# Attention of the 96-row heads: three key tiles to a turn in place of two

## The chip, the cores and the metric

The kernel runs on one core of a Trainium2 chip. The metric is the device time of one execution in microseconds (us), and of several executions the median. TensorE multiplies matrices, VectorE and ScalarE work elementwise and reduce, GpSimd (POOL) and SyncE (SP) here mostly issue transfers. TensorE's clock has two levels, 1.2 and 2.4 GHz; the profile gives the granted share of the higher one.

## The reference

A trunk of two layers works on 2048 latent tokens and 128 context tokens. In each layer one input projection feeds four groups of heads (latent attention, a state-space scan, a convolution module, grouped-query attention), whose outputs are gated and projected back. The change concerns the attention of the latent tokens to 128 context keys and 2048 latent keys, for four heads with 96 rows of query and key (64 plus 32 rotary) and four with 64:

```python
def one_block(qblk):
    s = jnp.einsum('bqgrd,bkgd->bgrqk', qblk, k).astype(jnp.float32) * scale
    p = jax.nn.softmax(s, axis=-1).astype(v.dtype)
    return jnp.einsum('bgrqk,bkgd->bqgrd', p, v)
```

## The kernel before

The function attention_phase runs once in each layer. Its unit is a block B: 1024 queries of one head, so two blocks for each of eight heads, 16 in a layer; blocks 0 to 7 are those of the 96-row heads (is_mla). A block walks over NKT = 17 tiles of 128 keys.

Each engine has its own program, written out in order, and they meet in semaphores. For a tile v of block B:

- scores(B, v) on TensorE: for a 96-row head six matmuls with 512 columns (two halves of the queries, three products each) into ST[unit % 2], two buffers of 1024 columns. It waits until the exponential of tile v - 2 has emptied its buffer.
- ScalarE takes the exponential of ST into Pb, five buffers. It waits until the value set and the sum of five tiles ago have used theirs.
- pv(B, v), the value set, on TensorE: the two query halves go side by side through two 64-column halves of the array into OT, in full float32. It waits for the exponential of its tile.
- add on VectorE sums the probabilities over the tiles into acc.

The exponential needs each query's maximum over all keys beforehand. So while block B is worked on, TensorE also computes raw scores of block B + 1 with queries on the partitions: fill(B + 1, r), r from 0 to 16, two matmuls with 512 columns (for r = 0, eight with 128) into the single buffer p1. VectorE reduces p1 to maxima. The next fill waits for it:

```python
out = p1
pe.wait_ge(q["red_done"], B * NKT + r + START)
```

VectorE's program takes, for each u from 0 to 16, reduce(B + 1, u) and then add(B, u - 1); behind u = 3 and 5 it sums the turned sums of block B - 1 (sum_keys), and in some blocks it splits a piece of the output weights behind u = 6 and 9.

TensorE's order in a block is the loop that the change touches: for u = 0, 2, 4, ... 16 a fill, the scores of tiles u and u + 1, some extra work, a second fill, and the value sets of tiles u - 2 and u - 1. At u = 0 the value set is that of tile 16 of the block before. Tile 16 has no second fill and no value sets; behind the loop come the value set of tile 14, max_row(B + 1) (eight transposes that make a row of the maxima) and the value set of tile 15. The extra work: turn_sums and turn transpose the sums and outputs of block B - 1 in turns u = 2, 4 and 6, and in blocks 0 and 1 of the first layer product does modulation rows for the next layer.

In block 0 no value set is carried over, so there the second fill of u = 0 and the first fill of u = 2 stand next to each other.

Of the kernel before, what the change touches and what calls it, by code (L numbers as in the profile page):

```python
# [29 lines left out]
DC = D // P  # L30
# [45 lines left out]
START = 1  # L76
# [1757 lines left out]
def attention_phase(nc, A, K, S, l, F, O, spare, M):  # L1834
# [7 lines left out]
    NKT = NLAT + 1  # L1842
# [10 lines left out]
    def is_mla(h):  # L1853
        return h < NMLA

    with ExitStack() as x:
# [27 lines left out]
        modulate = l == 0  # L1884
        if modulate:
            names += "bias_loaded m_used grown_ready m_row_ready g_stored m_stored m_loaded".split()
        q = {n: s.sem(n) for n in names}
# [3 lines left out]
        def loads(h, part):  # L1891
            return head_loads(l, h, part)
# [147 lines left out]
        def _(pe):  # L2040
            def fill(B, r):


                h, b = divmod(B, PER)
                par = h % 2
                if B == 0:
                    out = (p1, ST[1])[r % 2]
                    if r >= 2:
                        pe.wait_ge(q["red_done"], r - 1 + START)
                else:  # L2050
                    out = p1
                    pe.wait_ge(q["red_done"], B * NKT + r + START)
                if r == 0:
                    for i in range(NT_Q):
                        t = i // 2 + i % 2 * (NT_Q // 2)
                        q0 = b * QB + t * P
                        if is_mla(h):
                            qt, kt = Q1[par][0:QK, q0:q0 + P], K1[par][0:QK, LAT:KEYS]
                        elif t < NT_Q // 2:
                            qt, kt = Q1[par][0:HD, q0:q0 + P], K1[par][0:HD, LAT:KEYS]  # L2060
                        else:
                            qt, kt = Q2[par][HD:P, q0:q0 + P], K1[par][HD:P, LAT:KEYS]
                        mm = pe.matmul(out[:, t * P:(t + 1) * P], qt, kt, start=True, stop=True)
                else:
                    t, w = divmod(r - 1, WIDE)
                    q0 = b * QB + t * P
                    for c in range(2):
                        k0 = w * 1024 + c * 512
                        if is_mla(h):
                            qt, kt = Q1[par][0:QK, q0:q0 + P], K1[par][0:QK, k0:k0 + 512]  # L2070
                        elif c == 0:
                            qt, kt = Q1[par][0:HD, q0:q0 + P], K1[par][0:HD, k0:k0 + 512]
                        else:
                            qt, kt = Q2[par][HD:P, q0:q0 + P], K1[par][HD:P, k0:k0 + 512]
                        mm = pe.matmul(out[:, c * 512:(c + 1) * 512], qt, kt, start=True, stop=True)  # L2075
                mm.then_inc(q["p1_done"], 1)

            def context_scores():

                pe.wait_ge(q["c_summed"], 4 + START)  # L2080
                for h in range(NH):
                    rows = slice(0, QK if is_mla(h) else HD)
                    mm = pe.matmul(p1[:, h * P:(h + 1) * P], cQ[0][rows, h, :], cK[0][rows, h, :], start=True, stop=True)
                mm.then_inc(q["c_s_done"], 1)

            def context_turn():
                pe.wait_ge(q["c_e_ready"], NH + START)
                for h in range(NH):
                    mm = pe.transpose(p1[:, h * P:(h + 1) * P], cP[:, h, :], K.ident[:, :])
                mm.then_inc(q["c_t_done"], 1)  # L2090

            def context_values():
                pe.wait_ge(q["c_t_ready"], 1 + START)
                pe.wait_ge(q["c_v_loaded"], 16 + START)
                for h in range(NH):
                    mm = pe.matmul(p1[:, h * HD:(h + 1) * HD], cPT[:, h, :], cV[:, h, :], start=True, stop=True)
                mm.then_inc(q["c_pv_done"], 1)
# [29 lines left out]
            def turn(B):  # L2127

                pe.wait_ge(q["rden_ready"], B + 1 + START)
                pe.wait_ge(q["ot_copied"], B + 1 + START)  # L2130
                for t in range(4):
                    mm = pe.transpose(misc[:, t * P:(t + 1) * P], OTs[:, t * P:(t + 1) * P], K.ident[:, :])
                mm.then_inc(q["turned"], 1)

            def scores(B, kt):
                h, b = divmod(B, PER)
                par, unit = h % 2, B * NKT + kt
                ks = slice(kt * P, (kt + 1) * P)
                for half in range(2):
                    out = ST[unit % 2][:, half * 512:(half + 1) * 512]  # L2140
                    qs = slice(b * QB + half * 512, b * QB + half * 512 + 512)
                    if is_mla(h):
                        pe.matmul(out, K1[par][0:RM, ks], Q1[par][0:RM, qs], start=True, stop=False)
                        pe.matmul(out, K1[par][0:QK, ks], Q2[par][0:QK, qs], start=False, stop=False)
                        mm = pe.matmul(out, K2[par][0:QK, ks], Q1[par][0:QK, qs], start=False, stop=True)  # L2145
                    else:
                        pe.matmul(out, K1[par][:, ks], Q1[par][:, qs], start=True, stop=False)
                        mm = pe.matmul(out, K2[par][:, ks], Q2[par][:, qs], start=False, stop=True)  # L2148
                mm.then_inc(q["st_done"], 1)
# [11 lines left out]
            def product(k):  # L2161

                c = k % DC
                pe.wait_ge(M.w_loaded[c // 2], (64 if k < DC else 128) + START)
                if k == DC:
                    pe.wait_ge(q["o_ready"], 8 + START)
                M.product(pe, misc, c, [O.mod[:, c, 512 * j:512 * (j + 1)] for j in range(4)]).then_inc(q["m_used"], 1)

            pe.wait_ge(K.qk_loaded[0][0], loads(0, 0))
            for r in range(NKT):  # L2170
                fill(0, r)
# [3 lines left out]
            for B in range(NSB):  # L2175
                h, b = divmod(B, PER)
                last = B == NSB - 1
                pe.wait_ge(q["mrow_ready"], B + 1 + START)
                if b == 0:
                    pe.wait_ge(q[f"v_loaded{h % 2}"], 16 * (h // 2 + 1) + START)  # L2180
                if b == PER - 1 and not last:
                    for part in range(2):
                        pe.wait_ge(K.qk_loaded[(h + 1) % 2][part], loads(h + 1, part))
                    if h + 1 in (NMLA, NMLA + 1):
                        pe.wait_ge(q["ones_set"], h + 2 - NMLA + START)
                for u in range(0, NKT, 2):
                    if not last:
                        fill(B + 1, u)
                    for v in range(u, min(u + 2, NKT)):
                        if B * NKT + v >= 2:  # L2190

                            pe.wait_ge(q["exp_done"], B * NKT + v - 1 + START)
                        scores(B, v)
                    if last and u == 4:
                        context_scores()
                    elif last and u == 12:
                        context_turn()
                    elif last and u == 16:
                        context_values()
                    if modulate and B == 0 and u > DC:  # L2200
                        for c in range(u - DC - 2, u - DC):
                            product(c)
                    elif modulate and B == 1 and u >= 14:
                        for c in range(4):
                            product(DC + 2 * (u - 14) + c)
                    if u == 2 and B:
                        if modulate and B == 1:
                            pe.wait_ge(q["m_row_ready"], 4 + START)
                        elif modulate and B == 2:
                            pe.wait_ge(q["grown_ready"], 4 + START)  # L2210
                        turn_sums(B - 1, 0)
                    if u == 4 and B:
                        turn_sums(B - 1, 1)
                    if u == 6 and B:
                        turn(B - 1)
                    if u < NKT - 1 and not last:
                        fill(B + 1, u + 1)
                    if u == 0 and B:

                        pv(B - 1, NKT - 1)  # L2220
                    elif 0 < u < NKT - 1:
                        pv(B, u - 2)
                        pv(B, u - 1)
                pv(B, NKT - 3)
                if not last:
                    max_row(B + 1)
                pv(B, NKT - 2)
# [564 lines left out]
```

## Time and profile before

| | |
|---|---|
| median of 3 runs | 3855.65 us (3851.87 to 3858.28) |
| profiled execution | 3853.34 us |
| its span in the trace | 3851.2 us |
| TensorE busy | 3574.3 us, 93% |
| VectorE busy | 2909.7 us, 76% |
| ScalarE busy | 1496.6 us, 39% |

The span runs from the first to the last instruction of the program; the 2.1 us around it belong to the execution. In the rows below PE is TensorE (its matmuls), DVE VectorE, ACT ScalarE. A TensorE row gives line, operation and tile names: attn_p is p1 (a fill), attn_ST a score set, attn_OT a value set (its matmuls are recorded four to a tile), attn_misc a transposing of sums. attn_mx on VectorE is a reduce, attn_acc an add. A bracket at the end of a row gives the idle time ahead of it and what ended it. Ends of matmuls are modelled, so distances are best read from start to start.

### The profile page before, as it was taken

Reading aid. Unit: us, or ns where it says so; the run is one execution under the profiler, and the core shown is the slowest. Engines: PE = TensorE matmul, PEld = TensorE weight load, DVE = VectorE, ACT = ScalarE, POOL = GpSimd, SP = SyncE. Lnnn points to the kernel's source line nnn. Section 1 sums busy time; section 2 is a strip of 40 time slices with the busy share of each in tenths; the row PEclk is TensorE's granted clock in tenths of the full one; section 3 lists DMA queues with packets and bytes.
Section 4 is the critical chain, followed back from the end, with each engine's and each line's share of the span. In section 5 each row is a group of like instructions: output and inputs, shape, how many; then the busy total and the mean of one; then the engine's idle time right before and its main releaser. Section 6 shows DMA issues by size and latency. Waiting matters only on the chain. (4 is left out here: it accounts for less than half of the span.)

```text
span 3851.2 us, 50610 instructions
## 1 busy us (share of the span) xinstructions
PE 3574.3 (93%) x18001; PEld 2533.2 (66%) x18001; DVE 2909.7 (76%) x5064; ACT 1496.6 (39%) x3052; POOL 174.6 (5%) x263
## 2 busy tenths in 40 slices
PE   6999899598999999989969998995989999999899
PEld 5988788465555544548869887884656555544587
DVE  4539978687688798967745399786877777999676
ACT  5621134392344444441156211343923444444311
POOL 0000000001000000001000000000010000000010
PEclk8999999797999999989979999997979999999899
DMA  7535467616321222124455354676142221320243
GB/s 245 197 131 176 163 159 195 184 33 196 117 55 36 44 47 62 29 77 153 169 154 194 139 177 161 159 196 176 34 89 49 66 49 26 72 46 14 83 172 137
DMA packets 344772, 448.75 MB, mean 117 GB/s; under 512 B 136480, under 2 KB 275136, under 8 KB 327648
## 3 DMA queue, kind: packets, MB, share of 16 engines
q1 hardware_dynamic: 327328, 322.56, 27.5%
q0 software_dynamic: 17216, 123.22, 12.2%
q8 instruction: 134, 2.20, 0.2%
q14 instruction: 94, 0.77, 0.1%
HBM read 291.65 MB, written 154.04 MB: 116 GB/s over the span
## 5 line engine op out<-in xcount | busy, mean ns | idle before, releaser
L2288 ACT ACTIVATE attn_Pb<-attn_ST 128x1024 f32<-128x1024 f32 x544 | 547.1, 1026 | 849.6 <-PE attn_ST L2145 501.6
L2314 DVE TENSOR_REDUCE attn_mx<-attn_p 128x1 f32<-128x1024 f32 x496 | 605.5, 1221 | 211.9 <-PE attn_p L2075 205.7
L2370 DVE TENSOR_TENSOR attn_acc<-attn_acc,attn_Pb 128x1024 f32<-128x1024 f32 x480 | 584.0, 1217 | 24.0 <-ACT attn_Pb L2288 22.7
L2157 PE MATMUL attn_OT<-attn_Pb,attn_V 128*64 128x512 f32 x2176 | 536.6, 607 | 0.0
L592 PE MATMUL chan_b<-w_in_turned,w_in_hi 128*128 128x256 f32 (+1 forms) x1152 | 328.4, 285 | 17.6 <-DVE chan_hl L761 12.8
L593 PE MATMUL chan_b<-w_in_turned,w_in_lo 128*128 128x256 f32 (+1 forms) x1152 | 325.7, 283 | 0.0
L594 PE MATMUL chan_b<-chan_hl,w_in_hi 128*128 128x256 f32 (+1 forms) x1152 | 324.3, 282 | 0.0
L999 DVE SCALAR_TENSOR_TENSOR gate_GY<-gate_win,w_in_fw,gate_GY 128x1096 f32<-128x1096 f32 x240 | 311.5, 1364 | 0.4
L2157 PEld LDWEIGHTS attn_OT<-attn_Pb,attn_V 128*64 128x64 f32 x2176 | 127.9, 135 | 223.4 <-issue 179.0
L963 PE MATMUL gate_b<-w_in_hi,w_in_turned 128*128 128x512 f32 x544 | 216.9, 399 | 17.9 <-PEq L358 17.9
L592 PEld LDWEIGHTS chan_b<-w_in_turned,w_in_hi 128*128 128x128 f32 x1152 | 220.1, 191 | 19.8 <-DVE chan_hl L761 13.6
L594 PEld LDWEIGHTS chan_b<-chan_hl,w_in_hi 128*128 128x128 f32 x1152 | 221.7, 192 | 0.0
L593 PEld LDWEIGHTS chan_b<-w_in_turned,w_in_lo 128*128 128x128 f32 x1152 | 221.6, 192 | 0.0
L2554 PE MATMUL out_pY<-ahead_hi,out_oTh 128*128 128x512 f32 x544 | 221.3, 407 | 0.0
L964 PE MATMUL gate_b<-w_in_lo,w_in_turned 128*128 128x512 f32 x544 | 216.4, 398 | 0.0
L965 PE MATMUL gate_b<-w_in_hi,w_in_turned 128*128 128x512 f32 x544 | 216.4, 398 | 0.0
L2556 PE MATMUL out_pY<-ahead_hi,out_oTl 128*128 128x512 f32 x544 | 214.8, 395 | 0.0
L2148 PE MATMUL attn_ST<-attn_Q,attn_K 128*128 128x512 f32 x544 | 214.5, 394 | 0.0
L2555 PE MATMUL out_pY<-ahead_lo,out_oTh 128*128 128x512 f32 x544 | 213.5, 393 | 0.0
L974 ACT ACTIVATE gate_TH<-gate_b 128x512 f32<-128x512 f32 x68 | 40.7, 599 | 340.8 <-PE gate_b L965 340.8
L2075 PE MATMUL attn_p<-first_K,first_Q 96*128 96x512 f32 (+1 forms) x352 | 150.9, 482 | 9.7 <-DVE attn_mx L2314 9.0
L2075 PE MATMUL attn_p<-attn_K,attn_Q 96*128 96x512 f32 (+1 forms) x512 | 153.3, 464 | 5.0 <-DVE attn_mx L2314 5.0
(381 smaller groups left out, 7145.4 us busy)
## 6 DMA issues: line engine op xcount, KB each, us to landing
w_in_turned<-scratch_HT POOLq DMA_DIRECT2D x68, 1024.0 KB, 5.3
scratch_HT<-w_in_turned SPq DMA_DIRECT2D x34, 512.0 KB, 3.0
scratch_HT<-chan_hl SPq DMA_DIRECT2D x34, 512.0 KB, 4.3
scratch_G<-gate_GT SPq DMA_DIRECT2D x34, 512.0 KB, 2.7
out_G<-scratch_G SPq DMA_DIRECT2D x30, 512.0 KB, 4.8
scratch_QM<-head_QST SPq DMA_DIRECT2D x34, 384.0 KB, 3.6
scratch_KM<-head_KST SPq DMA_DIRECT2D x34, 384.0 KB, 4.8
w_in_raw<-in_w_in SPq DMA_DIRECT2D x96, 128.0 KB, 3.2
```

Of the source, the lines that this page charges most:

```text
L592: pe.matmul(dst, hi[:, c, cols], H, start=(c == 0), stop=False)
L593: pe.matmul(dst, lo[:, c, cols], H, start=False, stop=False)
L594: mm = pe.matmul(dst, hi[:, c, cols], L, start=False, stop=(c == DC - 1))
L963: pe.matmul(b[k % 8][:, :], H, hi[:, c, cols], start=(c == 0), stop=False)
L964: pe.matmul(b[k % 8][:, :], H, lo[:, c, cols], start=False, stop=False)
L999: ins = dve.scalar_tensor_tensor(y, win[i][:, f, k:k + WIN], fw[:, f, k:k + 1], y, ALU.mult, ALU.add)
L2075: mm = pe.matmul(out[:, c * 512:(c + 1) * 512], qt, kt, start=True, stop=True)
L2157: mm = pe.matmul(OT[o * HD:(o + 1) * HD, :], V[par][:, kt, :], Pb[unit % NPB][:, o * 512:(o + 1) * 512], start=(kt == 0), stop=(kt == NKT ...
L2288: act.activation(Pb[unit % NPB][:, :], ST[unit % 2][:, :], ACT.Exp).then_inc(q["exp_done"], 1)
L2314: ins = dve.tensor_reduce(mx[:, t, w:w + 1], made[:, :], AX.X, ALU.max)
L2370: ins = dve.tensor_tensor(sums[:, :], sums[:, :], prob[:, :], ALU.add)
L2554: pe.matmul(pY[par][:, cols], oTh[par][:, c, :], wh[:, c, cols], start=(c == 0), stop=False)
```

## The change

TensorE's loop is put into two functions. Blocks of 64-row heads (and so each layer's last block) run by_twos, which is the loop as it was. Blocks of 96-row heads run by_threes: two score sets first; then turns of three score sets followed by three value sets. The fills are placed anew: one ahead of each of the first two score sets of a turn and one behind its value sets; in the last turn one ahead of each score set. The first turn of threes has four value sets (tiles 0 to 3), the last has one (13), which stands next to that of tile 14. The extra work is tied to single tiles in behind. No instruction is added or removed, no buffer changes, and the programs of the other engines stay as they are.

```diff
+            def behind(B, v):
+                if modulate and B == 0 and v in (11, 13, 15, 16):
+                    for c in range(2 * (11, 13, 15, 16).index(v), 2 * (11, 13, 15, 16).index(v) + 2):
+                        product(c)
+                elif modulate and B == 1 and v >= 15:
+                    for c in range(4):
+                        product(DC + 4 * (v - 15) + c)
+                if v == 3 and B:
+                    sums_ready(B)
+                    turn_sums(B - 1, 0)
+                elif v == 5 and B:
+                    turn_sums(B - 1, 1)
+                elif v == 7 and B:
+                    turn(B - 1)
+
+            def by_threes(B):
+                fill(B + 1, 0)
+                for v in range(2):
+                    unit_scores(B, v)
+                fill(B + 1, 1)
+                if B:
+                    pv(B - 1, NKT - 1)
+                for u in range(2, NKT, 3):
+                    final = u == NKT - 3
+                    for v in range(u, u + 3):
+                        if v < u + 2 or final:
+                            fill(B + 1, v)
+                        unit_scores(B, v)
+                        behind(B, v)
+                    for v in range(u - 1 if u > 2 else 0, u if final else u + 2):
+                        pv(B, v)
+                    if not final:
+                        fill(B + 1, u + 2)
...
-                for u in range(0, NKT, 2):
-                    if not last:
-                        fill(B + 1, u)
-                    for v in range(u, min(u + 2, NKT)):
-                        if B * NKT + v >= 2:
-                            pe.wait_ge(q["exp_done"], B * NKT + v - 1 + START)
-                        scores(B, v)
...
-                    if u < NKT - 1 and not last:
-                        fill(B + 1, u + 1)
-                    if u == 0 and B:
-                        pv(B - 1, NKT - 1)
-                    elif 0 < u < NKT - 1:
-                        pv(B, u - 2)
-                        pv(B, u - 1)
+                if is_mla(h):
+                    by_threes(B)
+                else:
+                    by_twos(B, last)
                 pv(B, NKT - 3)
                 if not last:
                     max_row(B + 1)
```

## Rows read from the trace of the kernel before

**Rows 1.** the page, parts 1 and 2: busy us (share) xinstructions; granted clock in 40 slices

```profile
PE 3574.3 (93%) x18001; PEld 2533.2 (66%) x18001; DVE 2909.7 (76%) x5064; ACT 1496.6 (39%) x3052; POOL 174.6 (5%) x263
...
PEclk8999999797999999989979999997979999999899
```

**Rows 2.** windows: a 96-row and a 64-row block; busy us per engine, granted clock

```profile
1201.86:1254.78 52.92, 52.52 (x231) 31.62 (x231) 42.43 (x39) 22.32 (x29) 3.04 (x2) 1.00 0.03 5
1359.72:1403.65 43.93, 43.53 (x196) 21.64 (x196) 39.97 (x37) 19.81 (x27) 3.89 (x7) 1.00 0.45 93
```

**Rows 3.** waits of TensorE, then VectorE, in 1201.86:1254.78; us in total, times, longest

```profile
PE attn_p L2075 <- DVE attn_mx L2314: 0.3, 1, 0.3
...
DVE attn_mx L2314 <- PE attn_p L2075: 8.5, 10, 2.1
```

**Rows 4.** timeline of TensorE, one pair of tiles; start us, us, instruction

```profile
1232.10 0.74 PE L2075 MATMUL attn_p<-attn_K,attn_Q 96*128 96x512 f32 x2
1232.68 0.40 PE L2143 MATMUL attn_ST<-first_Q,first_K 97*128 97x512 f32 x1
...
1235.48 0.62 PE L2075 MATMUL attn_p<-attn_K,attn_Q 96*128 96x512 f32 x2
1236.03 1.94 PE L2157 MATMUL attn_OT<-attn_Pb,attn_V 128*64 128x512 f32 x8
1237.90 0.50 PE L2075 MATMUL attn_p<-attn_K,attn_Q 96*128 96x512 f32 x1
```

**Rows 5.** timeline of TensorE, one block's end and the next one's start

```profile
1198.63 1.08 PE L2157 MATMUL attn_OT<-attn_Pb,attn_V 128*64 128x512 f32 x4
1199.63 1.12 PE L2104 MATMUL attn_p<-ident,attn_mtm 128*97 128x128 f32 x8
...
1201.86 1.11 PE L2063 MATMUL attn_p<-attn_K,attn_Q 96*128 96x128 f32 x8
...
1205.65 0.62 PE L2075 MATMUL attn_p<-attn_K,attn_Q 96*128 96x512 f32 x2
...
1207.59 0.72 PE L2075 MATMUL attn_p<-attn_K,attn_Q 96*128 96x512 f32 x2 [0.31 <-DVE attn_mx L2314]
1208.15 0.39 PE L2143 MATMUL attn_ST<-first_Q,first_K 97*128 97x512 f32 x1
```

**Rows 6.** timeline of VectorE, the same block's first tiles

```profile
1206.31 1.22 DVE L2314 TENSOR_REDUCE attn_mx<-attn_p 128x1 f32<-128x1024 f32 x1 [2.08 <-PE attn_p L2075]
1208.35 1.23 DVE L2314 TENSOR_REDUCE attn_mx<-attn_p 128x1 f32<-128x1024 f32 x1 [0.82 <-PE attn_p L2075]
1209.49 1.22 DVE L2368 TENSOR_TENSOR attn_acc<-attn_Pb 128x1024 f32<-128x1024 f32 x1
```

**Rows 7.** timeline of TensorE, a pair with a turning of sums, fill to fill

```profile
1213.82 0.73 PE L2075 MATMUL attn_p<-attn_K,attn_Q 96*128 96x512 f32 x2
...
1220.06 0.73 PE L2075 MATMUL attn_p<-attn_K,attn_Q 96*128 96x512 f32 x2
```

**Rows 8.** timeline of TensorE, block 0 of the first layer, two adjacent fills

```profile
925.56 0.62 PE L2075 MATMUL attn_p<-first_K,first_Q 96*128 96x512 f32 x2
927.50 0.73 PE L2075 MATMUL attn_p<-first_K,first_Q 96*128 96x512 f32 x2 [1.32 <-DVE attn_mx L2314]
...
928.82 0.63 PE L2145 MATMUL attn_ST<-first_Q,attn_K 96*128 96x512 f32 x1
929.25 0.63 PE L2143 MATMUL attn_ST<-first_Q,first_K 97*128 97x512 f32 x1
```

**Rows 9.** windows: the stretch with that idle, and the one behind it

```profile
924.80:928.20 3.40, 2.08 (x9) 1.40 (x9) 1.23 (x1) 1.13 (x2) 2.98 (x3) 1.00 0.91 180
928.20:931.60 3.40, 3.40 (x10) 2.63 (x9) 3.19 (x2) 0.84 (x1) 2.10 (x2) 0.50 1.02 433
```

**Rows 10.** timeline of TensorE, heads phases: idles at full clock

```profile
493.96 0.42 PE L1189 MATMUL head_bL<-ident,head_ql 128*96 128x128 f32 x2 [1.30 <-DVE head_ck L1272]
...
2629.43 1.53 PE L1168 MATMUL head_bU<-head_wuq,head_LT 96*128 96x384 f32 x4 [1.22 <-ACT head_LT L1233]
```

More of the change, by code:

```diff
@@ L2167, in product, with unit_scores, sums_ready @@
                 M.product(pe, misc, c, [O.mod[:, c, 512 * j:512 * (j + 1)] for j in range(4)]).then_inc(q["m_used"], 1)
+            def unit_scores(B, v):
+                if B * NKT + v >= 2:
+                    pe.wait_ge(q["exp_done"], B * NKT + v - 1 + START)
+                scores(B, v)
+            def sums_ready(B):
+                if modulate and B == 1:
+                    pe.wait_ge(q["m_row_ready"], 4 + START)
+                elif modulate and B == 2:
+                    pe.wait_ge(q["grown_ready"], 4 + START)
@@ new lines, in by_twos @@
+            def by_twos(B, last):
+                for u in range(0, NKT, 2):
+                    if not last:
+                        fill(B + 1, u)
+                    for v in range(u, min(u + 2, NKT)):
+                        unit_scores(B, v)
+                        behind(B, v)
+                    if last and u == 4:
+                        context_scores()
+                    elif last and u == 12:
+                        context_turn()
+                    elif last and u == 16:
+                        context_values()
+                    if u < NKT - 1 and not last:
+                        fill(B + 1, u + 1)
+                    if u == 0 and B:
+                        pv(B - 1, NKT - 1)
+                    elif 0 < u < NKT - 1:
+                        pv(B, u - 2)
+                        pv(B, u - 1)
@@ L2185, in _ @@
                         pe.wait_ge(q["ones_set"], h + 2 - NMLA + START)
-                for u in range(0, NKT, 2):
-                    if not last:
-                        fill(B + 1, u)
-                    for v in range(u, min(u + 2, NKT)):
-                        if B * NKT + v >= 2:
-                            pe.wait_ge(q["exp_done"], B * NKT + v - 1 + START)
-                        scores(B, v)
[L2194 to L2215, printed above, removed]
-                    if u < NKT - 1 and not last:
-                        fill(B + 1, u + 1)
-                    if u == 0 and B:
-                        pv(B - 1, NKT - 1)
-                    elif 0 < u < NKT - 1:
-                        pv(B, u - 2)
-                        pv(B, u - 1)
+                if is_mla(h):
+                    by_threes(B)
+                else:
+                    by_twos(B, last)
                 pv(B, NKT - 3)
```

## The prediction

> **What bounds the kernel now.** I read the page first. TensorE is busy for 93% of the span, and its granted clock stands at full through the slices of both attention phases [rows 1]. Then I cut the span by stage. One block of a 96-row head (1024 queries against 17 key tiles) takes 52.92 us, with TensorE busy for 52.52 of it and VectorE for 42.43, at granted clock 1.00; a block of a 64-row head takes 43.93 us [rows 2]. There are eight of the first kind in each of the two layers, 16 in all. So the changed stage is bound by TensorE alone. The view of waits says the same: in that block TensorE waits once, for 0.3 us, and VectorE waits ten times, 8.5 us in all, for fills [rows 3]. The reader is to see there which way slack runs: VectorE has some, TensorE has none, so whatever makes TensorE wait is paid in full.
>
> The order of TensorE's timeline shows why so little is lost [rows 4]. A pair of tiles goes: fill, two score sets, fill, two value sets. A fill always has either 2.80 us of scores or 1.87 us of values behind it before the next fill. That matters because p1 is one buffer: fill r waits for the count red_done of reduce r-1. A reduce starts 0.76 us after the start of its fill, and the next fill can start 1.28 us after the start of the reduce (1206.31 to 1207.59) [rows 5, 6]. Two fills can therefore not start closer together than 2.04 us. In a pair they are 3.38 and 2.42 us apart [rows 4].
>
> **The change part by part: what it removes.** In twos, a block has ten runs of value sets (the carried one, seven pairs, and two single ones around max_row). In threes it has seven (the carried one, one of four, three of three, one of two, one single). A run costs more than its value sets: one alone takes 1.00 us, 1198.63 to 1199.63 [rows 5], two take 1.87 [rows 4], so each further one is 0.87 and 0.13 is for the run. The fill behind a run takes 0.58 and that in front of one 0.55, where two matmuls at the scores' spacing (2.80 us for 12) would take 0.47 [rows 4]; that is 0.11 and 0.08 more. Together a run costs 0.32 us. Three fewer in 16 blocks are 48 x 0.32 = 15 us saved.
>
> **What it adds.** Follow the order written out in by_threes. A turn u ends with fill(u + 2), and the next turn begins with fill(u + 3). Between these two fills stands nothing. It happens for fills 4 and 5, 7 and 8, 10 and 11, 13 and 14: four times a block, 64 times in all. Set the first of them at 0. VectorE is idle by then (below), so its reduce starts at 0.76, and the second fill starts at 2.04 instead of 0.56 (a fill to the work behind it, 1207.59 to 1208.15 [rows 5]): 1.48 us of waiting. The trace of before has this very pattern once in each layer, in block 0, where no carried value set stands between fills 1 and 2: the fills start 1.94 us apart (925.56, 927.50), with TensorE idle for 1.32 [rows 8]. What is queued behind the waiting fill is the whole turn: its three score sets, and behind these ScalarE's exponentials and VectorE's adds, so nothing else moves up meanwhile.
>
> The wait goes on into the turn. Scores begin at 2.60 and take 1.40, so the third fill is wanted at 4.00. VectorE goes from reduce to add in 1.14 us [rows 6]; its next reduce comes behind that add, at 3.04, and the third fill may start at 4.32. That is 0.32 of waiting, and 0.09 because a fill that waited takes 0.56 and not 0.47. Then scores 4.88 to 7.68, 0.08 before a run, three value sets 0.13 + 3 x 0.87 = 2.74: the turn ends at 10.50. Three tiles by pairs take 1.5 x 5.80 = 8.70 [rows 4]. The turn of three is 1.80 longer although it saves run costs.
>
> The cover on VectorE: behind the reduce at 3.04 come an add (4.18), a reduce (5.32) and an add (6.46 to 7.68). The next turn's first reduce is at 11.26, so 3.6 us lie idle, which also hold the splitting operation of some blocks. ScalarE is busy for 22.32 us of the block [rows 2], and a value set always follows its own score set by at least one further score set or value set, so I price waits for probabilities at nothing; without that cover one costs what is left of an exponential, about a microsecond.
>
> **The block summed.** Fill 0 to fill 2 is as before, 1201.86 to 1207.59: 5.73 [rows 5]. A block-end turning of sums costs 0.44 (a pair with one takes 6.24 [rows 7] against 5.80).
> - Fill 2 to fill 4: scores end at 1.96; fill 3 may start at 2.04; scores from 2.60 to 4.00, a turning, scores to 5.84, four value sets 3.61 and 0.08: 9.53.
> - Fill 4 to fill 7: 10.50, plus two turnings, the first of which hides the 0.41: 10.97.
> - Fill 7 to 10, and 10 to 13: 2 x 10.50 = 21.00.
> - Fill 13 to the end: the last turn has a fill ahead of each score set, so VectorE's 2.28 for a reduce and an add sets their pace: fills at 2.04, 4.32 and 6.60, scores to 8.56, two value sets to 10.51; from max_row to the next fill 0 it is 2.23 as before (1199.63 to 1201.86): 12.74.
>
> That is 59.97 against 52.92, or 7.05 a block and 113 us for 16. The profiled execution took 3853.34, so at full clock it would be 3966. The median of the runs shown is 2.3 above that execution.
>
> Of the moved parts (products of the modulation, turnings of sums), each keeps its tile or moves by one; they issue the same instructions, no DMA is moved, SP and POOL keep their orders, and POOL's loads of a next head, which wait for the scores of the head before, come as much later as their users. A product that lands in front of a waiting fill hides up to 0.41; in two blocks that is under 2 us, and I leave it out.
>
> **The clock, which the trace prices only from far.** At the one place with two adjacent fills at full clock, the granted clock was 1.00 in the stretch that holds the idle 1.32 us, and 0.50 in the 3.4 us behind it [rows 9]. In these, scores start 0.43 apart [rows 8] instead of 0.233. The fall cost 3.4 x (1 - 0.233 / 0.43) = 1.56 us. Against that stand three idles of 1.22 to 1.30 us in the heads phases, behind which the clock stayed at full [rows 10]: one of the first kind shown, two of the second (one in each layer). So the bounds are no fall, 0 us, and one for each of 64 stalls, 100 us. One in four of the like idles fell, but it is the one with exactly this pattern; between 0.25 and 1 I take 0.4, or some 26 falls. Half of them should swallow the 0.41 behind them, so one costs 1.35 net: 35 us.
>
> The Trainium skill speaks both ways here. Its page "TensorE: Matmul & The Clock Gate", section "Why this matters for your kernels", names only idle gaps longer than these stalls as what brings the clock down; by that rule the sum stays at 3966. Its section "A second HAM failure mode: psum-queue depth-cycling" tells of frequent short idles between groups of matmuls that make the clock swing, which would give 3966 and up to 100 more. The row of block 0 goes with the second, the rows of the heads phase with the first.
>
> Forecast: 3966 + 35 + 2 for the median, about 4003.
>
> **The rivals.**
> - The clock stays full throughout: 3966 to 3968. For it, the idles of the heads phases [rows 10]; against it, block 0 [rows 9]. This is also what the skill's first rule gives.
> - The clock falls behind nearly every stall, or VectorE is late as well: 4066 if each stall costs 1.56. If VectorE still held an add when the first fill lands, each stall would be up to 1.14 longer, 73 us more. Against that, the 3.6 us of idle time worked out above.
> - It ends faster: only the 48 saved runs count, 3838. That needs the adjacent fills to cost nearly nothing. It decides once a stall is under 0.96 / 4 = 0.24 us, that is when a reduce is done before its follower is wanted. Against it is the 1.32 idle of block 0 [rows 8], where code and buffers are the same.
> - The change does less than it says, with part of the stalls covered by drift between VectorE and TensorE: 3880 to 3950. I find no work that could cover them, since both fills stand next to each other in one engine's order.
>
> **Chances and range.** Forecast (falls behind some stalls, 3985 to 4055): 0.60. Clock full, 3950 to 3985: 0.22. Falls nearly everywhere or VectorE late, above 4055: 0.11. Stalls partly covered: 0.04. Faster: 0.02; no change, 0.01. The range 3955 to 4062 holds the first, most of the second and the edge of the third, a little over 8 in 10. A measurement of this kernel can tell about 0.2% (8 us) from no change; by that bound faster is 0.02, same 0.01, slower 0.97.
>
> **What would show it.** In the profile of the changed kernel: TensorE's view of waits has, in a 96-row block, four waits of about 1.3 us and about five short ones for the reduce, in place of one of 0.3; the block takes 60 us where the clock stays full and 62 to 63 where it falls twice; VectorE's and TensorE's instruction counts are unchanged; a middle run of three value sets takes 2.7 us; blocks of 64-row heads stay at 43.93; the granted clock of the stage shows short stretches at 0.5. It is wrong if the blocks stay under 56 us (then something covers the reduce), or if they pass 65 (then the clock stays low or another wait has come, a probability or a value set).

## The result and the profile after

The changed kernel takes 4026.76 us, median of four runs (4009.12 to 4028.05), against 3855.43 for the kernel before: ratio 1.0433 from all the runs (the two medians alone give 1.0444), 95% interval 1.041 to 1.0455. It is slower by 171 us, inside the predicted range and 24 us above the predicted time. The profiled execution took 4026.34 us, 173.0 more than that of before.

The windows of the two stages with 96-row heads, first in the kernel before (one row a layer; span, busy us of TensorE, its weight loads, VectorE, ScalarE, POOL, with the count of instructions behind each; then the granted clock, the DMA share and GB/s):

```profile
919.24:1359.72 440.48, 436.24 (x1952) 253.85 (x1952) 336.32 (x310) 169.32 (x215) 18.93 (x22) 0.99 0.28 81
2841.40:3268.84 427.44, 423.20 (x1825) 252.84 (x1825) 330.27 (x301) 169.33 (x215) 18.92 (x22) 0.98 0.19 44
```

The same stages of the changed kernel, three single 96-row blocks, a 64-row block, and two turns of three tiles:

```profile
921.57:1448.64 527.07, 477.61 (x1952) 271.92 (x1952) 332.91 (x310) 169.85 (x215) 19.83 (x23) 0.92 0.24 68
2930.20:3442.04 511.84, 461.83 (x1824) 270.35 (x1824) 326.73 (x301) 169.86 (x215) 20.66 (x23) 0.92 0.16 37
1067.24:1131.77 64.53, 58.45 (x231) 33.78 (x231) 42.20 (x40) 22.47 (x29) 0.00 (x0) 0.92 0.28 78
1131.77:1194.27 62.50, 56.52 (x231) 33.73 (x231) 42.12 (x39) 22.36 (x29) 2.01 (x4) 0.95 0.12 31
1255.43:1322.82 67.39, 61.34 (x230) 35.80 (x231) 42.11 (x39) 22.57 (x29) 3.90 (x3) 0.87 0.02 4
1492.58:1536.52 43.94, 43.53 (x198) 21.63 (x198) 39.97 (x37) 19.84 (x27) 2.79 (x6) 1.00 0.07 16
1093.51:1104.01 10.50, 9.04 (x39) 5.07 (x37) 8.03 (x7) 3.79 (x7) 0.00 (x0) 1.00 0.06 12
1104.01:1119.03 15.02, 13.70 (x38) 7.35 (x36) 6.98 (x6) 3.89 (x7) 0.00 (x0) 0.66 0.27 82
```

The stages grew by 86.6 and 84.4 us, 171.0 of the 173.0. The 64-row block stayed at 43.94 [rows 2]. TensorE's instruction count in a block is as before and VectorE's busy time (42.1 to 42.2) nearly so, so the new time is not new work. TensorE was busy for 52.52 of 52.92 us [rows 2] and is now for 56.52 of 62.50: it idles for 6.0 us in place of 0.4, and the same instructions take 4.0 longer. The two turns show why: with the same instructions one takes 10.50 us at granted clock 1.00 and the other 15.02 at 0.66. The clock is the second loss beside the waiting.

The view of waits of TensorE in the block 1067.24 to 1131.77, answering to [rows 3]:

```profile
PE attn_p L2075 <- DVE attn_mx L2352: 5.6, 5, 1.3
```

These are the four long waits and, as before, one of 0.3 at the start of the block. The short waits of the third fills, of which the prediction expected about five in this view, are not counted in it; they show in the starts below.

Then the timeline of TensorE (fills and value sets of the turn at full clock; scores left out) and that of VectorE, answering to [rows 4, 6]:

```profile
1093.51 0.73 PE L2075 MATMUL attn_p<-attn_K,attn_Q 96*128 96x512 f32 x2
1095.56 0.73 PE L2075 MATMUL attn_p<-attn_K,attn_Q 96*128 96x512 f32 x2 [1.32 <-DVE attn_mx L2352]
...
1097.82 0.73 PE L2075 MATMUL attn_p<-attn_K,attn_Q 96*128 96x512 f32 x2
...
1101.28 2.79 PE L2157 MATMUL attn_OT<-attn_Pb,attn_V 128*64 128x512 f32 x12
1104.01 0.73 PE L2075 MATMUL attn_p<-attn_K,attn_Q 96*128 96x512 f32 x2
```

```profile
1094.28 1.23 DVE L2352 TENSOR_REDUCE attn_mx<-attn_p 128x1 f32<-128x1024 f32 x1 [2.17 <-PE attn_p L2075]
1095.42 1.22 DVE L2408 TENSOR_TENSOR attn_acc<-attn_acc,attn_Pb 128x1024 f32<-128x1024 f32 x1
1096.55 1.22 DVE L2352 TENSOR_REDUCE attn_mx<-attn_p 128x1 f32<-128x1024 f32 x1
...
1104.78 1.22 DVE L2352 TENSOR_REDUCE attn_mx<-attn_p 128x1 f32<-128x1024 f32 x1 [2.48 <-PE attn_p L2075]
```

Read the starts. The two adjacent fills are 2.05 us apart, with TensorE idle for 1.32 until the reduce of 1094.28 is done. The third fill starts 2.26 behind the second, because its reduce (1096.55) stands behind an add. The values take 2.73 and the turn 10.50. That is the worked-out turn to the hundredth; inside it the two distances came as 2.05 and 2.26, worked out as 2.04 and 2.28.

### The profile page after: what moved, and what is told of

Same layout as the page of the kernel before. It is cut to its first block and busy times, and to the rows that moved or that the text cites. A ratio compares the mean times of both kernels' runs of the same rounds, so it can differ in the third digit from the quotient of the medians.

```text
span 4024.2 us, 50610 instructions
## 1 busy us (share of the span) xinstructions
PE 3655.2 (91%) x18001; PEld 2567.6 (64%) x18001; DVE 2903.0 (72%) x5064; ACT 1500.6 (37%) x3052; POOL 175.9 (4%) x263
## 5 line engine op out<-in xcount | busy, mean ns | idle before, releaser
L2075 PE MATMUL attn_p<-attn_K,attn_Q 96*128 96x512 f32 (+1 forms) x512 | 162.6, 482 | 50.1 <-DVE attn_mx L2352 47.1
L2075 PEld LDWEIGHTS attn_p<-attn_K,attn_Q 96*128 96x128 f32 (+1 forms) x512 | 65.5, 192 | 185.8 <-DVE attn_mx L2352 139.5
```

## The experiments

Two theories were set against each other. Mine: two fills next to each other on one buffer p1 wait for a reduce, and the idle brings the clock down behind some of these waits. The rival: the grouping by three is at fault, with three score sets on two buffers ST and three value sets on five buffers Pb. A second question is how much of the loss is waiting and how much is clock.

**The last fill of a turn in front of its values.** The turns of three stay.

```diff
+                    if not final:
+                        fill(B + 1, u + 2)
                     for v in range(u - 1 if u > 2 else 0, u if final else u + 2):
                         pv(B, v)
-                    if not final:
-                        fill(B + 1, u + 2)
```

> The three-tile turns stay; only the last fill of each turn moves from behind its value sets to in front of them, so that no two fills stand next to each other. If adjacent fills behind one buffer p1 are the cause (waits of 1.32 us and the clock falls behind them), the 64 long waits vanish, a middle turn takes 8.70 us instead of 10.50, a 96-row block about 52.8 us, the clock stays full in the stage, and the time is 3850 to 3856 us. If turns of three score sets and three value sets are themselves the cause (ST with two buffers, Pb with five), it stays near 4027.

Measured: 3856.06 us against 3854.36, ratio 1.0002 (0.9993 to 1.0011). One such block, in windows:

```profile
1096.83:1149.80 52.97, 52.44 (x231) 31.70 (x231) 42.11 (x39) 22.34 (x29) 2.00 (x4) 1.00 0.13 38
```

Grouping by three costs nothing by itself; the place of one fill is worth the whole 171 us. A turn of this run, its first two fills and the next turn's first, and the reduce that the second waits for:

```profile
1121.95 0.72 PE L2075 MATMUL attn_p<-first_K,first_Q 96*128 96x512 f32 x2
1123.99 0.74 PE L2075 MATMUL attn_p<-first_K,first_Q 96*128 96x512 f32 x2
...
1130.64 0.72 PE L2075 MATMUL attn_p<-first_K,first_Q 96*128 96x512 f32 x2
```

```profile
1122.71 1.22 DVE L2352 TENSOR_REDUCE attn_mx<-attn_p 128x1 f32<-128x1024 f32 x1 [0.58 <-PE attn_p L2075]
```

The turn takes 8.69 us, where three tiles by pairs take 8.70, although it has fewer runs of value sets. The middle fill starts 2.04 behind the first, right behind the end of the reduce, so no room is left there. The next run gives the middle fill more.

**All fills spread.** The middle fill also moves, between the two halves of the second score set.

```diff
...
                 for half in range(2):
+                    if half and middle is not None:
+                        fill(B + 1, middle)
...
-                        if v < u + 2 or final:
+                        if v == u:
                             fill(B + 1, v)
-                        unit_scores(B, v)
+                        unit_scores(B, v, v if v == u + 1 else None)
                         behind(B, v)
+                    fill(B + 1, u + 2)
                     for v in range(u - 1 if u > 2 else 0, u if final else u + 2):
                         pv(B, v)
-                    if not final:
-                        fill(B + 1, u + 2)
```

> As the run with the fill in front of the values, and the middle fill of a turn stands between the two halves of the second score set, so that fills are at least 2.5 us apart; in the last turn too the third fill stands in front of the values. By the adjacent-fill theory no fill waits any more, a middle turn takes 8.54 us, a block about 52.0 us (three runs of value sets fewer at 0.32 us each), and the time is 3838 to 3842 us, 0.4% under the kernel before. If the runs of value sets are worth nothing, it is 3853 to 3856; if grouping by three is the cause of the loss, near 4027.

Measured: 3840.4 us against 3854.36, ratio 0.9959 (0.9945 to 0.9973): 0.4% under the kernel before, and clear of the interval. A block of it in windows, and one turn in TensorE's timeline:

```profile
1146.87:1198.64 51.77, 51.37 (x231) 32.09 (x231) 42.56 (x39) 22.34 (x29) 0.00 (x0) 1.00 0.34 85
```

```profile
1171.79 0.72 PE L2075 MATMUL attn_p<-first_K,first_Q 96*128 96x512 f32 x2
...
1174.45 0.62 PE L2075 MATMUL attn_p<-first_K,first_Q 96*128 96x512 f32 x2
...
1177.01 0.62 PE L2075 MATMUL attn_p<-first_K,first_Q 96*128 96x512 f32 x2
1177.56 2.79 PE L2159 MATMUL attn_OT<-attn_Pb,attn_V 128*64 128x512 f32 x12
1180.29 0.72 PE L2075 MATMUL attn_p<-first_K,first_Q 96*128 96x512 f32 x2
```

Fills stand 2.66, 2.56 and 3.28 us apart, all above 2.04, and none of this turn waits; the turn takes 8.50 (forecast 8.54). The block is 1.15 shorter than before, of which three runs of value sets at the predicted 0.32 would be 0.96. Over the kernel 14 us came of it, 0.29 for each of 48 runs if all of it is put down to them; this run does not part them from the new places of the fills.

**Pairs with adjacent fills.** The grouping of before, the 96-row blocks alone with the second fill behind the values.

```diff
-                    if u < NKT - 1 and not last:
+                    behind_values = is_mla(B // PER)
+                    if u < NKT - 1 and not last and not behind_values:
                         fill(B + 1, u + 1)
...
+                    if u < NKT - 1 and behind_values:
+                        fill(B + 1, u + 1)
...
-                if is_mla(h):
-                    by_threes(B)
-                else:
-                    by_twos(B, last)
+                by_twos(B, last)
```

> The kernel before with pairs of tiles; in the 96-row blocks alone the second fill of a turn moves behind the value sets, next to the first fill of the next turn: eight adjacent pairs a block instead of four. By the adjacent-fill theory a pair takes 7.36 us instead of 5.80, a block 65 us, 4047 us at full clock, and more with clock falls: 4050 to 4150. If turns of three are the cause, pairs stay near 5.8 us and the time near 3855.

Measured: 4139.11 us against 3854.36, ratio 1.0745 (1.0727 to 1.0763). A pair at full clock in TensorE's timeline, from one first fill to the next:

```profile
1276.42 0.73 PE L2075 MATMUL attn_p<-first_K,first_Q 96*128 96x512 f32 x2
1278.47 0.74 PE L2075 MATMUL attn_p<-first_K,first_Q 96*128 96x512 f32 x2 [1.32 <-DVE attn_mx L2352]
...
1281.95 1.94 PE L2157 MATMUL attn_OT<-attn_Pb,attn_V 128*64 128x512 f32 x8
1283.82 0.73 PE L2075 MATMUL attn_p<-first_K,first_Q 96*128 96x512 f32 x2
```

The same 2.05 and 1.32, without any turn of three; 7.40 a pair (forecast 7.36) and twice as many pairs, hence a larger loss than that of the change. The record of the granted clock has a fall to 0.50 behind 45 of the 128 pairs: 36 of 3.4 us and 9 of 6.8. The rival is out from both sides.

**TensorE kept busy in the wait.** The changed kernel; the score set that follows the second adjacent fill is computed once more ahead of it and overwritten later (told=False keeps the extra set from being counted). The output is not affected.

```diff
...
+                        if v == u and u > 2:
+                            pe.wait_ge(q["exp_done"], B * NKT + v - 1 + START)
+                            scores(B, v, told=False)
                         if v < u + 2 or final:
                             fill(B + 1, v)
```

> The changed kernel, with the score set of the next tile computed twice: once more in front of the second of two adjacent fills, where TensorE waits anyway (six matmuls, 1.4 us, overwritten by the real set). The wait stays, the idle goes. If the loss is 113 us of waiting plus some 58 us of clock falls, the clock stays full, turns take 10.5 to 10.6 us throughout, and the time is 3965 to 3972 us. If the granted clock has nothing to do with the idle (or is a mere sign of something else), it stays at 4027 or above.

Measured: 3969.29 us against 3854.36, ratio 1.0293 (1.0277 to 1.0309). TensorE's timeline at one such pair of fills (of the extra set the first and the last matmul), and the block in windows:

```profile
1204.55 0.73 PE L2075 MATMUL attn_p<-first_K,first_Q 96*128 96x512 f32 x2
1205.12 0.40 PE L2143 MATMUL attn_ST<-first_Q,first_K 97*128 97x512 f32 x1
...
1206.30 0.39 PE L2145 MATMUL attn_ST<-first_Q,attn_K 96*128 96x512 f32 x1
...
1206.60 0.73 PE L2075 MATMUL attn_p<-first_K,first_Q 96*128 96x512 f32 x2
```

```profile
1178.30:1238.30 60.00, 59.09 (x254) 36.05 (x254) 41.93 (x39) 22.35 (x29) 0.00 (x0) 1.00 0.31 76
```

The fills are still 2.05 us apart, six matmuls more are done between them, and the kernel is 57 us faster than the changed one. The block takes 60.00 us (forecast 59.97). So 115 us are waiting, less what the saved runs give, and the other 57 are the clock: more work at the same place gave time back.

**Less of it: one and two matmuls in the wait.** In place of the whole set, one matmul with 512 columns into the same buffer; the run with two has range(2).

```diff
+                        if v == u and u > 2:
+                            pe.wait_ge(q["exp_done"], B * NKT + v - 1 + START)
+                            par, qs = B // PER % 2, slice(B % PER * QB, B % PER * QB + 512)
+                            for _ in range(1):
+                                pe.matmul(ST[(B * NKT + v) % 2][:, 0:512], K1[par][0:QK, v * P:(v + 1) * P], Q1[par][0:QK, qs], start=True, stop=True)
```

> The changed kernel with one matmul of 512 columns, overwritten later, between the two adjacent fills, where TensorE waits: the waits for the reduce stay as long in start-to-start terms (2.05 us), the idle shrinks from 1.32 to about 1.1 us. If the clock's share of the loss hangs on how long TensorE idles, it falls less often than the 21 times of the changed kernel: 3966 to 3995 us. If a wait at this place brings the clock down whatever its length, the time stays at 4009 to 4028.

> The same with two matmuls, so that some 0.85 us of idle is left in each of the 64 waits. By the idle theory no falls or very few: 3966 to 3972 us, as with six. Otherwise 4009 to 4028.

Measured: 3967.9 us with one (ratio 1.0294, 1.0278 to 1.0309) and 3969.32 with two (1.0304, 1.0288 to 1.032), both against 3855.22. The second of two adjacent fills in the run with one matmul, and a stretch of two blocks in its windows:

```profile
1145.90 0.73 PE L2075 MATMUL attn_p<-first_K,first_Q 96*128 96x512 f32 x2 [1.08 <-DVE attn_mx L2357]
```

```profile
1177.57:1297.57 120.00, 109.43 (x468) 64.50 (x468) 83.86 (x78) 44.69 (x58) 3.89 (x3) 1.00 0.16 40
```

One matmul, which takes 0.23 us at the spacing of the scores and leaves an idle of 1.08 in place of 1.32, gives back as much as six. The lower end of the expectation came out: in the profiled execution the clock fell behind none of these 64 shortened waits. The same holds for the one with two.

**One adjacent pair a block.** The kernel with spread fills, fill 10 put back behind the values of its turn (the edit is against that kernel).

```diff
-                    fill(B + 1, u + 2)
+                    if u != 8:
+                        fill(B + 1, u + 2)
                     for v in range(u - 1 if u > 2 else 0, u if final else u + 2):
                         pv(B, v)
+                    if u == 8:
+                        fill(B + 1, u + 2)
```

> The kernel with all fills spread (3840 us), with one adjacent pair put back in each 96-row block: fill 10 behind its value sets and next to fill 11. Each of the 16 pairs should cost 1.5 us of waiting: 24 us, 3864 at full clock. If a third of the stalls bring the clock down, as in the changed kernel, at 2.7 us each, 14 us more: 3875 to 3885. If falls come only where stalls follow each other closely, 3864; if each isolated stall brings one, about 3905.

Measured: 3881.93 us against 3855.22, ratio 1.0069 (1.0055 to 1.0082). A block without a fall and one with a fall in windows, then the stretches inside the second around the fall:

```profile
1264.24:1317.63 53.39, 51.67 (x230) 32.01 (x231) 40.36 (x37) 20.44 (x27) 2.51 (x5) 1.00 0.37 77
1099.43:1154.37 54.94, 53.22 (x230) 33.17 (x231) 42.56 (x39) 22.33 (x29) 2.00 (x4) 0.97 0.15 39
1134.46:1136.00 1.54, 1.54 (x7) 1.27 (x8) 1.54 (x2) 0.00 (x0) 0.00 (x0) 1.00 0.00 0
1136.00:1139.40 3.40, 3.40 (x10) 2.66 (x9) 2.04 (x3) 1.02 (x1) 0.00 (x0) 0.50 0.00 0
1139.40:1150.00 10.60, 10.60 (x47) 6.91 (x45) 9.00 (x8) 4.87 (x9) 0.00 (x0) 1.00 0.42 113
```

A block in which no fall came takes 53.39 us, one with a fall of 3.4 us 54.94. So the adjacent pair by itself costs 53.39 - 51.77 = 1.62 and the fall 1.55, against 1.5 and 1.56 worked out beforehand. The clock fell behind 10 of the 16 pairs, for 3.4 us behind 8 of them. Isolated stalls bring it down too. The time lies in the range that was written for falls behind a third of the pairs at 2.7 us each; it is made up of more falls that cost less, so that this range held was luck.

**The short second wait taken away.** The 64 adjacent pairs stay; the middle fill goes between the halves of the second score set, as in the kernel with spread fills (not shown again), and in the last turn the third fill stands in front of the values.

```diff
...
-                        if v < u + 2 or final:
+                        if v == u:
                             fill(B + 1, v)
-                        unit_scores(B, v)
+                        unit_scores(B, v, v if v == u + 1 else None)
                         behind(B, v)
+                    if final:
+                        fill(B + 1, u + 2)
```

> The changed kernel with its 64 adjacent pairs kept, and the second, short wait of each turn taken away (the middle fill between the halves of the second score set, and in the last turn the third fill in front of the values). At full clock a middle turn takes 10.1 us instead of 10.5 and a block about 58.4 us: 3942 us without falls. If the short wait is what makes falls of the changed kernel last 6.8 and 10.2 us, the falls here last 3.4 us as with one adjacent pair, and come behind some 6 of 10 stalls (40 x 1.55): about 4005 us. If their length has another cause, long ones remain, and the time is anywhere from 3990 to 4020; if falls come as often as in the changed kernel but short, 3975.

Measured: 3952.59 us against 3857.73, ratio 1.0247 (1.023 to 1.0264), below all three cases that I had written down. Two blocks and the fall in the second, in windows:

```profile
1117.51:1175.69 58.18, 52.51 (x231) 31.89 (x231) 42.36 (x39) 22.35 (x29) 2.01 (x4) 1.00 0.14 36
...
1057.54:1117.51 59.97, 54.30 (x231) 32.94 (x231) 45.05 (x44) 22.35 (x29) 0.00 (x0) 0.97 0.29 81
1087.20:1090.60 3.40, 3.40 (x10) 2.62 (x9) 2.01 (x2) 1.02 (x1) 0.00 (x0) 0.50 0.00 0
```

The second fill of a pair in TensorE's timeline:

```profile
1145.60 0.73 PE L2075 MATMUL attn_p<-first_K,first_Q 96*128 96x512 f32 x2 [1.32 <-DVE attn_mx L2356]
```

At full clock the block is as worked out (58.18 against 58.4). But the clock fell behind only 6 of the 64 waits, each time for 3.4 us. My guess of 40 short falls was wrong, although each wait was still 1.32 us.

## Why the prediction was right, and by how much its clock term was off

- **What bounds.** Right: TensorE alone. VectorE's work in a block stayed at 42 us, and all that TensorE waited for lengthened the block. One reading was loose: the clock is not full in the first slice of either attention phase [rows 1], and the two stages have 0.99 and 0.98.
- **The runs saved.** 0.32 us each was worked out; the kernel with spread fills gives 0.29 if its whole gain is theirs. That the changed kernel saves as much under its loss is likely, since it has the same runs, but no run shows it by itself.
- **The adjacent fills.** Right in place, number and size: 2.05 and 1.32 us, turn 10.50 at full clock, block 60.00 against 59.97 in the kernel that kept TensorE busy, and 115 us against 113 in the sum. Only the bound was put too strictly: two fills can start closer than 2.04 us, as the 1.94 of [rows 8] had shown.
- **The clock.** The mechanism was right, the size was not: 35 us were put in, some 57 came. The step "some 26 falls" of "1.35 net" was off in both factors. In the record of the granted clock the stages of the changed kernel have 19 stretches at 0.50 behind the 64 new pairs (two more stand behind the pairs in block 0, one in each layer, which the change did not make). They are fewer than the 26 and much longer: 3 of 3.4 us, 8 of 6.8 and 8 of 10.2, in all 147 us or 7.7 a fall. I had the length of one fall from one row [rows 9], 3.4 us. 57 / 19 is 3.0 us a fall, more than twice what I took. The two errors partly offset each other, so the forecast came nearer than its clock term deserved.
- **A sign of being wrong that came.** The prediction named a block above 65 us as one, because then the clock stays low or another wait has come. Such blocks came: the one of 67.39 us above, at granted clock 0.87, has falls of 6.8 and 10.2 us in it. It was the first of the two named causes: the clock stayed low for longer than the 3.4 us that the sum had for a fall.
- **What a fall's length hangs on** is not settled. Where no second wait stood in the turn, most falls lasted 3.4 us: all 6 above, 8 of the 10 behind single pairs, and 36 of the 45 in the kernel with pairs. The others lasted 6.8 us, and one 10.2. That goes with the second wait as the cause of the longest ones; it doesn't show it, since the timing of the turns changed as well, and some falls were long without it. How often the clock falls behind the same 1.32 us (19 of 64, 6 of 64, 10 of 16, 45 of 128) is open too.
- **The rivals.** A full clock throughout is what the kernel with one extra matmul got, 3968 as the rival said; the changed kernel did not. VectorE was not late: its first reduce in a turn came out of 2.17 and 2.48 us of idle time. That stalls are covered or the saved runs win needed other places for the fills, and with these the saved runs won, at 3840 against the 3838 named.

## What to carry to other kernels

Where one engine fills a single buffer and another empties it, write down the distance from fill to fill that the pair of them needs (here 1.94 to 2.05 us), and keep that much other work between any two fills when an order is regrouped: the seam from one turn to the next counts as well as the inside. Regrouping paid 14 us once the fills were spread evenly, and cost 171 with two of them at a seam. If such a wait can't be avoided on TensorE, a matmul that is thrown away can be cheaper than idling, as it was here.

## What the runs showed of the hardware

Idle time of 1.32 us on a TensorE that is otherwise at work was followed in some cases (19 of 64 in the changed kernel) by a stretch at granted clock 0.50, the 1.2 GHz level, of 3.4 to 10.2 us. One throw-away matmul in each wait (idle 1.08 us) was followed by none in 64, and the kernel took 59 us less for 64 matmuls of 0.23 us. The Trainium skill's page "TensorE: Matmul & The Clock Gate", in its section "Why this matters for your kernels", names only longer gaps; by that the clock would have stayed full, and here it did not, so the measurement decides. Its section "A second HAM failure mode: psum-queue depth-cycling" tells of short idles between groups of matmuls that make the clock swing, and the changed kernel with its 19 falls agrees with that; the run with idles of 1.08 us, as many of them, shows no fall.
